# Turning the feed-forward activations on TensorE instead of VectorE

## What is computed

```
def second_block(x, ...):                      # the first block ends alike, with a shift and gates
    ...
    x = x + rms_norm_2(mix, norm_mix_post[l])
    hn = rms_norm_2(x, norm_ffn_pre[l])
    f = (jax.nn.silu(hn @ w_gate[l]) * (hn @ w_up[l])) @ w_down[l]
    x = x + rms_norm_2(f, norm_ffn_post[l])
```

## Time and profile before

| | us |
|---|---|
| median of 3 runs (lowest, highest) | 2594.59 (2592.34, 2597.17) |
| the profiled execution | 2597.17 |
| its span, first to last instruction | 2595.4 |
| TensorE busy | 2545.3 (98%) |
| VectorE busy | 1836.3 (71%) |
| ScalarE busy | 1276.5 (49%) |

### The profile page before, as it was taken

How to read it: one execution, slowest core, us unless ns; L and a number is a source line. 1 busy time by engine, 2 the same in 40 slices (tenths; PEclk the granted TensorE clock), 3 DMA queues, 4 the chain that set the end, 5 groups by cost and what they waited for, 6 DMA issues and landing times.

```text
span 2595.4 us, 28953 instructions
## 1 busy us (share of the span) xinstructions
PE 2545.3 (98%) x11478; PEld 2086.3 (80%) x11478; DVE 1836.3 (71%) x2267; ACT 1276.5 (49%) x1753; POOL 3.9 (0%) x11
## 2 busy tenths in 40 slices
PE   7999999999999999999999999999999999999998
PEld 5888777878878888888888787788788888888886
DVE  7999899989887777557766645666666665456665
ACT  4445767754454444444444555554554444444443
POOL 0000000000000000000000000000000000000000
PEclk9999999999999999999999999999999999999999
DMA  9998456877956566666555554445455555555553
GB/s 376 363 345 310 157 208 212 291 287 268 387 193 227 211 227 243 243 227 226 198 213 190 179 178 170 167 174 188 176 187 195 188 209 194 195 193 195 193 196 130
DMA packets 80569, 578.12 MB, mean 223 GB/s; under 512 B 8990, under 2 KB 9254, under 8 KB 10673
## 3 DMA queue, kind: packets, MB, share of 16 engines
q1 hardware_dynamic: 78768, 566.92, 59.9%
q10 hardware_dynamic: 1154, 6.67, 0.6%
q0 software_dynamic: 512, 2.69, 0.3%
HBM read 574.13 MB, written 3.68 MB: 223 GB/s over the span
## 4 chain that ended last, share of the span: by engine, by line
PE 87%; DVE 6%; ACT 3%; DMA 2%; issue 1%; DVEq 0%; ACTq 0%; SPq 0%
PE bank L695 83%; DVE wlo L1523 2%; DMA raw<-in_w_o 1%; ACT whi L1003 1%; DVE raw L1533 1%; DMA raw<-in_w_in 1%; PE bank L647 1%; DVE X L1518 1%; PE bank L808 0%; ACT SS L1179 0%; PE bank L791 0%; PE bank L733 0%; PE bank L927 0%; PE bank L856 0%; DVE SC L1680 0%
## 5 line engine op out<-in xcount | busy, mean ns | idle before, releaser
L1523 DVE TENSOR_TENSOR wlo<-raw,whi 128x1024 fp32r<-128x1024 f32 x882 | 1073.6, 1223 | 695.8 <-ACT whi L1003 692.4
L1003 ACT ACTIVATE whi<-raw 128x1024 fp32r<-128x1024 f32 x882 | 931.5, 1059 | 1176.9 <-PE bank L695 1051.5
L695 PE MATMUL bank<-whi,HTh 128*128 128x512 f32 x2560 | 699.5, 395 | 7.1 <-ACT HTh L1003 5.8
L695 PE MATMUL bank<-wlo,HTh 128*128 128x512 f32 x2560 | 688.0, 390 | 6.1 <-DVE wlo L1523 6.1
L695 PE MATMUL bank<-whi,HTl 128*128 128x512 f32 x2560 | 688.1, 390 | 0.8 <-DVE HTl L1518 0.7
L695 PEld LDWEIGHTS bank<-wlo,HTh 128*128 128x128 f32 x2560 | 481.5, 188 | 109.6 <-DVE wlo L1523 8.9
L695 PEld LDWEIGHTS bank<-whi,HTl 128*128 128x128 f32 x2560 | 481.9, 188 | 104.4 <-DVE HTl L1518 1.6
L695 PEld LDWEIGHTS bank<-whi,HTh 128*128 128x128 f32 x2560 | 474.3, 189 | 107.8 <-issue 9.2
L1533 DVE CUSTOM_DVE_ANT_0 raw<-raw,GT,VECS 128x2048 f32<-128x2048 f32 x96 | 224.7, 2345 | 0.3 <-DMA raw<-in_w_ada 0.3
L695 PE MATMUL bank<-whi,ACTh 128*128 128x512 f32 x704 | 190.1, 391 | 0.0
L695 PE MATMUL bank<-wlo,ACTh 128*128 128x512 f32 x704 | 188.8, 389 | 0.0
(11 more groups left out here) (229 smaller groups left out, 1187.7 us busy)
## 6 DMA issues: line engine op xcount, KB each, us to landing
raw<-in_w_in SPq DMA_DIRECT2D x128, 1024.0 KB, 4.9
raw<-in_w_ada SPq DMA_DIRECT2D x96, 1024.0 KB, 6.0
raw<-in_w_gate SPq DMA_DIRECT2D x88, 1024.0 KB, 4.8
raw<-in_w_up SPq DMA_DIRECT2D x88, 1024.0 KB, 4.8
raw<-in_w_down SPq DMA_DIRECT2D x88, 1024.0 KB, 4.8
raw<-in_w_o SPq DMA_DIRECT2D x16, 1024.0 KB, 7.2
raw<-in_w_out SPq DMA_DIRECT2D x16, 1024.0 KB, 4.8
raw<-in_w_attn_out SPq DMA_DIRECT2D x8, 1024.0 KB, 4.8
```

The lines of the kernel that those rows point to most:

```text
L695: i = e.matmul(bank[2 * ch.st + t][:, :], (xl if ps == 1 else xh)[:, k, tk(t)], (lo if ps == 2 else hi)[:, j * 512:j * 512 + 512], start=c ...
L1003: return e.activation(dst, src, ACT.Copy, scale=scale)
L1523: e.tensor_tensor(lo, src, r32(hi), S_).then_inc(lo_done, 1)
```

## The change

The 16 transposes of 32 x 32 blocks of each chunk leave VectorE. In their place TensorE turns the product over, four transposes of 128 x 128 for each half `t`, into bank 6 + t, ahead of the pieces 18 and 19 of the chunk, counted from its first gate piece. ScalarE's copy to `ACTh` and VectorE's subtraction to `ACTl` read that bank, one half at a time. `SG` and `FT` go: the silu results now go round six buffers `stg` of 512 columns in the same place. The waits of the readers and writers follow, and so do `gt_row` and `gt_diagonals` of the second row, which now use `stg[0]` and `stg[1]`.

```diff
-    f_items = [(p, c) for p in R(2) for c in R(FCUT[p][1] // 4)]
-    f_turn = [steps(f"f{n}_turn", [(p, c, i) for p, c in f_items for i in R(16)]) for n in R(2)]
+    f_items = [[(p, c, t) for p in R(2) for c in R(FCUT[p][1] // 4) for t in R(2)] for _ in R(2)]
+    f_pe = [steps(f"f{n}_pe", f_items[n]) for n in R(2)]
...
 # tensor, gained(n, q)
             elif n == 1:
+                w.wait_ge(*f_dve[0](1, 4, 1))
                 w.wait_ge(*row_dve(1, 3))
...
 # tensor
+        def act_t(n, part, c, t):
+            b = bank[6 + t]
+            ch = next(x for x in P.chunks if x.kind == "up" and x.j == (n, part, c))
+            w.wait_ge(emptied["DVE"], ch.emptied[t])
+            before = f_items[n].index((part, c, t)) - 2
+            if before >= 0:
+                w.wait_ge(*f_dve[n](*f_items[n][before]))
+            else:
+                for i in R(12, 16):
+                    w.wait_ge(*part_act[2 * n](i))
+                w.wait_ge(*(g_dve[2](15) if n else m_dve("lo", 14)))
+            transposes(b, stg[(2 * c + t) % 6], 4).then_inc(*f_pe[n].one(part, c, t))
+            yield 1
...
+        for n in R(2):
+            for part, c, t in f_items[n]:
+                lane.begin(M[f"ffn{n}{part}"] + 16 * c + 18 + t, act_t(n, part, c, t))
...
 # scalar, evict, a gate chunk
-                    gate_free(n, part, c)
-                    e.activation(SG[:, t, :], B[:, :], ACT.Silu,
+                    gate_free(n, part, c, t)
+                    e.activation(stg[(2 * c + t) % 6][:, :], B[:, :], ACT.Silu,
...
-        def gate_free(n, part, c):
-            if c:
-                w.wait_ge(*f_turn[n](part, c - 1, 15))
+        def gate_free(n, part, c, t):
+            if c >= 3:
+                w.wait_ge(*f_pe[n](part, c - 3, t))
             elif part:
-                w.wait_ge(*f_turn[n](0, FCUT[0][1] // 4 - 1, 15))
+                w.wait_ge(*f_pe[n](0, 3 + c, t))
...
-        def turned(n, part, c):
-            w.wait_ge(*f_turn[n](part, c, 15))
+        def act_t(n, part, c, t):
+            w.wait_ge(*f_pe[n](part, c, t))
             if c == 0:
                 w.wait_ge(pe_done, M[f"ffn{n}{part}"])
-            copy(ACTh[:, 4 * c:4 * c + 4, :], FT[:, :, :]).then_inc(*f_act[n].one(part, c))
+            copy(ACTh[:, 4 * c:4 * c + 4, tk(t)], tri(bank[6 + t][:, :], 4)).then_inc(*f_act[n].one(part, c, t))
...
 # vector
-        def turned(n, part, c, ops):
-            before = f_items.index((part, c)) - 1
...
-            for i in R(16):
-                f, k = slice(32 * (i // 4), 32 * (i // 4) + 32), slice(32 * (i % 4), 32 * (i % 4) + 32)
-                src = SG[k, :, :].rearrange("p t (b c) -> p t b c", b=4)[:, :, :, f]
-                dst = FT[f, :, :].rearrange("p b (t c) -> p t b c", t=2)[:, :, :, k]
-                e.transpose(dst, src).then_inc(*f_turn[n].one(part, c, i))
-                if i % ops == ops - 1:
-                    yield 1
-            yield 1
+        def act_t(n, part, c, t):
+            w.wait_ge(*f_act[n](part, c, t))
             hs = slice(4 * c, 4 * c + 4)
-            w.wait_ge(*f_act[n](part, c))
-            e.tensor_tensor(ACTl[:, hs, :], FT[:, :, :], r32(ACTh[:, hs, :]), S_).then_inc(*f_dve[n].one(part, c))
+            e.tensor_tensor(ACTl[:, hs, tk(t)], tri(bank[6 + t][:, :], 4), r32(ACTh[:, hs, tk(t)]), S_).then_inc(
+                *f_dve[n].one(part, c, t))
```

More of the change, by code:

```diff
@@ L321, in build @@
     stg = [at(f"stg{i}", 75776 + 2048 * i, [512]) for i in range(6)]
-    SG = at("SG", 75776, [2, 512])
-    FT = at("FT", 75776 + 4096, [4, T])
     ACTh = at("ACTh", 0, [ACTK, T], f32r)
@@ L456, in build @@
     g_dve = [None] + [steps(f"g{n}_dve", list(R(16))) for n in (1, 2)]
-    f_items = [(p, c) for p in R(2) for c in R(FCUT[p][1] // 4)]
-    f_turn = [steps(f"f{n}_turn", [(p, c, i) for p, c in f_items for i in R(16)]) for n in R(2)]
-    f_act = [steps(f"f{n}_act", f_items) for n in R(2)]
-    f_dve = [steps(f"f{n}_dve", f_items) for n in R(2)]
+    f_items = [[(p, c, t) for p in R(2) for c in R(FCUT[p][1] // 4) for t in R(2)] for _ in R(2)]
+    f_pe = [steps(f"f{n}_pe", f_items[n]) for n in R(2)]
+    f_act = [steps(f"f{n}_act", f_items[n]) for n in R(2)]
+    f_dve = [steps(f"f{n}_dve", f_items[n]) for n in R(2)]
     TJ2 = [(n, j, t) for n in ("q", "k") for j in R(2) for t in R(2)]
@@ L530, in wait_hi @@
         else:
-            w.wait_ge(*f_act[int(x[1])](int(x[2]), k // 4))
+            w.wait_ge(*f_act[int(x[1])](int(x[2]), k // 4, 1))
     def wait_lo(w, x, k):
@@ L554, in wait_lo @@
         else:
-            w.wait_ge(*f_dve[int(x[1])](int(x[2]), k // 4))
+            w.wait_ge(*f_dve[int(x[1])](int(x[2]), k // 4, 1))
     TJ_SRC = {"qi0": (stg[4], stg[5]), "k4": (stg[4], stg[5]), "qi4": (PART[0][:, 0, :], PART[0][:, 1, :]),
@@ L591, in dif_bank @@
         return {"L0": (7, 6), "L1": (5, 5), "TR": (7, 5), "PV": (7, 6), "OT0": (7, 5), "OT1": (7, 6)}[k][t]
-    def turn_slot(n, part, c):
-        last = c == FCUT[part][1] // 4 - 1
-        return M[f"ffn{n}{part}"] + 16 * c + 17, 4 if last else 2
     def rows_of(n, j, t):
@@ L732, in gt_row @@
                 w.wait_ge(*gt_act(n, j, 3))
-                e.matmul(bank[4][:, :], ones[:, :], stg[4 * n + j % 2][:, :], start=True, stop=True).then_inc(
-                    *gt_pe.one(n, j))
+                e.matmul(bank[4][:, :], ones[:, :], stg[j % 2][:, :], start=True, stop=True).then_inc(*gt_pe.one(n, j))
                 yield 2
@@ L1081, in evict @@
                     i = 2 * j + t
-                    w.wait_ge(*f_dve[n](1, 4))
+                    w.wait_ge(*f_pe[n](1, 4, 1))
                     if n == 0:
@@ L1254, in gt_diagonals @@
                 elif n:
-                    w.wait_ge(*part_pe[0](14))
-                    w.wait_ge(*sq_act[0](3, 1))
+                    w.wait_ge(*f_pe[0](1, 3, 1))
                 else:
@@ L1260, in gt_diagonals @@
                 for i in R(4):
-                    copy(stg[4 * n + j % 2][:, i * 128:i * 128 + 128], ident[:, :], GTC[:, n, 4 * j + i:4 * j + i + 1]).then_inc(
+                    copy(stg[j % 2][:, i * 128:i * 128 + 128], ident[:, :], GTC[:, n, 4 * j + i:4 * j + i + 1]).then_inc(
                         *gt_act.one(n, j, i))
@@ L1484, in scalar @@
         for n in R(2):
-            for part, c in f_items:
-                at_slot, ops = turn_slot(n, part, c)
-                lane.begin(at_slot + 16 // ops, turned(n, part, c))
+            for part, c, t in f_items[n]:
+                lane.begin(M[f"ffn{n}{part}"] + 16 * c + 18 + t, act_t(n, part, c, t))
         for i, (name, j, t) in enumerate(TJ2):
@@ L1614, in evict @@
                     n, part, c = ch.j
-                    sg = SG[:, t, :]
+                    sg = stg[(2 * c + t) % 6][:, :]
                     w.wait_ge(*summed(ch, t))
@@ L2071, in vector @@
         for n in R(2):
-            for part, c in f_items:
-                at_slot, ops = turn_slot(n, part, c)
-                lane.begin(at_slot, turned(n, part, c, ops))
+            for part, c, t in f_items[n]:
+                lane.begin(M[f"ffn{n}{part}"] + 16 * c + 18 + t, act_t(n, part, c, t))
         lane.begin(B1 + 10, pad2())
```

## The result

The changed kernel takes 2615.66 us (median of 4 runs, 2615.18 to 2617.14), the kernel before 2595.28 us (4 runs). The ratio is 1.0084, with a 95% interval of 1.0072 to 1.0095. By the medians it is 20.4 us slower, where 21.1 us and 2615.7 us were forecast. Of 24 executions of the changed kernel on record, 23 lie between 2613.00 and 2621.79 us (median 2616.59, 21.3 us above 2595.28), and one took 3215.61 us at a granted clock of 0.752 and is left out.

What follows compares the result with a forecast made beforehand. TensorE, never idle in the FFNs, was taken as the bound: 22 pairs of transpose groups at 0.96 us add 21.1 us to 2594.6, everything else 0, giving 2615.7 us, range 2609 to 2625.

Steps and rivals of the forecast that it cites:

- The bound: Both FFNs: TensorE never idles, so the end moves one for one with its work; VectorE's time is worth nothing.
- The price: TensorE in the FFNs: 44 groups of four transposes, 22 pairs at 0.96 us, 21.1 us.
- The bounds: Limits on the transposes' price: 15.4 us if only 0.35 us a group counts, 47.9 us if transposes do not overlap.
- the rival of 2610.0 us: TensorE's groups: only the next matmul's 0.35 us later start counts, 44 times, 15.4 us; chance 4%.
- What VectorE and ScalarE get: 44 bank-reading subtractions (30.1 us) and 44 copies (25.8 us); VectorE loses 150 us in all; both count 0.
- The margin of the added wait: TensorE's group, ahead of piece 18, waits for its half's product, done 4.4 and 4.3 us earlier: cost 0.
- the rival of the late product: TensorE's groups wait for VectorE's multiplications, 1.28 or 1.40 us a chunk, some 29.5 us: 2645.2 us; chance 6%.
- Giving back ScalarE's wait: FFNs: silu's 40.2 us of waiting for VectorE's turns had delayed TensorE and is returned: 2575.5 us; chance 2%.
- Hidden transposes: TensorE in the FFNs: transposes slip in among matmuls as weight loads do, no change, 2594.6 us; chance 2%.
- the start-only price: TensorE's groups cost only the next matmul's later start, 44 x 0.35 us: 2610.0 us; chance 4%.
- Waiting for the product: TensorE's groups stand idle until VectorE's multiplications end, some 29.5 us over 22 chunks: 2645.2 us; chance 6%.
- the falling clock: Each pair of groups drops TensorE to 1.2 GHz for a while, 35.2 us more: 2650.9 us; chance 2%.

Runs made afterwards that it cites:

- e6_slot17: The changed kernel with the groups of transposes one piece earlier, ahead of pieces 17 and 18: 2630.41 us, ratio 1.0127.
- e2_both: The kernel before, VectorE's transposes kept, with TensorE's 44 groups of four transposes added in the change's slots, result unread: 2615.36 us, ratio 1.0076.
- e7_slot16: The changed kernel with the groups two pieces earlier, ahead of pieces 16 and 17: 2709.78 us, ratio 1.0435.
- e3_twice: The changed kernel with each group of four transposes done twice, eight in a row into the same bank: 2640.36 us, ratio 1.0165.

## Why the prediction was right

**The bound.** TensorE's chain without a gap in both FFNs made its own instructions the price of the change. Right: with 138 us of VectorE's work gone nothing moves, with TensorE's groups added to it everything does.

**The price.** 0.96 us for a pair, read over whole pieces, against 0.97 measured; 21.1 us against 21.3 in the two FFNs. The bounds held as bounds. The reading of the lower one, 0.35 us for four starts, was wrong: it is the distance from the first transpose to the next matmul, and holds three distances between transposes and a short one. It moved only the rival of 2610.0 us, and the runs show that no group of four costs so little.

**What VectorE and ScalarE get.** 44 subtractions of 683 and 44 copies of 587 ns were taken from the earlier trace rows. After:

```profile
L1920 DVE TENSOR_TENSOR ACTl<-bank,ACTh 128x512 fp32r<-128x512 f32 x44 | 30.1, 684 | 0.4 <-ACT ACTh L1014 0.4
L1014 ACT ACTIVATE ACTh<-bank 128x512 fp32r<-128x512 f32 x44 | 25.6, 581 | 0.2 <-PE bank L641 0.2
```

684 and 581 ns; 150 us less were forecast for VectorE, and 148.2 came. Both on the path for 0, as forecast.

**The margin of the added wait: wrong.** The prediction put it at 4.4 and 4.3 us. In the changed kernel the products are made here:

```profile
789.33 1.28 DVE L1631 TENSOR_TENSOR stg<-bank,stg 128x512 f32<-128x512 f32 x2
...
2054.65 1.40 DVE L1527 SCALAR_TENSOR_TENSOR stg<-bank,SUMS,stg 128x512 f32<-128x512 f32 x2
```

They end at 790.61 and 2056.05. The groups begin at 792.28 (above) and here:

```profile
2057.60 0.60 PE L641 MATMUL bank<-ident,stg 128*128 128x128 f32 x4
```

That is 1.67 and 1.55 us. The step that failed was to take the row at 796.53 for the start of piece 18. Most likely the product, at 790.87, was taken to follow at once on the end of the last up piece, and the pieces were counted from there; the prediction does not say how they were counted. But VectorE makes the split of its slot first, and the product only behind it: in the changed kernel piece 16 begins at 792.28 - 2 x 2.72 = 786.84, 2.49 us before the product. From the product's start to the first group it is 792.28 - 789.33 = 2.95 us in the changed kernel, so in the trace of before the place was near 790.87 + 2.95 = 793.82, and a piece does begin there, one ahead of the row that was taken:

```profile
793.81 1.07 PE L695 MATMUL bank<-whi,HTh 128*128 128x512 f32 x4
```

With 1.6 us of margin the cost is 0 all the same, but the working did not secure that zero: its count was off by a piece and happened not to matter. And the distance to the rival of the late product was overstated by a whole piece: one piece less, and it costs 13 us in the FFNs, as e6_slot17 shows.

**The rivals.** Giving back ScalarE's wait: refuted by e2_both, where it is there in full at the same time. Hidden transposes and the start-only price: refuted by the chain. Waiting for the product and the falling clock: neither is there in the changed kernel (no idle in the FFNs, clock 1.00). The wait is real one piece earlier (e6_slot17), the fall two pieces earlier, in ten chunks of 22 (e7_slot16). With eight transposes in a row, in e3_twice, the granted clock of both FFNs is 1.00 still. The Trainium skill ("TensorE: Matmul & The Clock Gate", Part 4: PE-mode transpose) says that transposes do not count as work for the clock gate; groups of eight among matmuls, 0.79 us long, did not bring the clock down here, and no run tells whether they count.

No version here beats the kernel before: all that were tried with the transposes on TensorE are slower. What points further, giving VectorE the transposes that TensorE still does elsewhere, was not tried, and whether it would gain is open.

## What to carry to other kernels

Before work is moved between engines, look at the idle time of the receiving engine in that very stretch, not at the busy shares: here 148 us taken from an engine with slack were worth nothing (e2_both still has them, and its FFNs take the same time to 0.1 us), and 21 us given to the one without slack cost 21.3. Price an instruction that is put into a full pipeline from start to start over whole units of work around a place that already does it; durations overstate it (272 ns shown, 0.12 us paid for each of four), and the gap to the next start understates it. Where a wait is added, find the release by its own event and count the margin in the order of the program from there, since a margin that is one piece too large looks just as safe. A wait costs more than its idle time: 0.22 us more here, and more again where the clock falls.

## What the runs showed of the hardware

A 128 x 128 float32 transpose among matmuls of 512 columns costs TensorE 0.11 us, and a group of them 0.04 us once; the duration shown is 272 ns each. Matmuls kept their 0.2267 us from start to start with VectorE's transposes beside them or not. A wait cost 0.22 us beyond the idle time shown: 0.16 us in which the next instruction would have started before the shown end of the last matmul, and some 0.06 us of slower start. After waits of 0.35 to 0.63 us, 21 times, that was all, and the granted clock was 1.00 over both FFNs (e6_slot17). After waits of 3.07 to 3.35 us the granted clock fell in ten chunks (0.50 to 0.74 over the 3 us from the group's start) and stayed at 1.00 in twelve (e7_slot16).
